# Seven block products for the up projection as well, and whole-block factors for the down projection

## The reference

```python
h = rms_norm(x, norm_ffn[l])                                  # 512 x 1024
x = x + jnp.square(jax.nn.relu(h @ w_up[l])) @ w_down[l]      # w_up 1024 x 4096, w_down 4096 x 1024
```

## Time and profile before

| | |
|---|---|
| median of three runs | 967.56 us |
| the profiled execution's own time | 967.63 us |
| its span, first to last instruction | 965.8 us |
| TensorE busy, matmuls | 954.9 us, 99% of the span, 4624 of them |
| VectorE busy | 599.3 us, 62% |
| ScalarE busy | 486.2 us, 50% |
| GpSimd busy | 168.6 us, 17% |
| moved by DMA | 116.18 MB, mean 120 GB/s |
| mean granted clock of TensorE | 0.999 |

### The profile page before, as it was taken

How to read it: one execution, slowest core, us unless ns; L and a number is a source line. 1 busy time by engine, 2 the same in 40 slices (tenths; PEclk the granted TensorE clock), 3 DMA queues, 4 the chain that set the end, 5 groups by cost and what they waited for, 6 DMA issues and landing times.

```text
span 965.8 us, 11653 instructions
## 1 busy us (share of the span) xinstructions
PE 954.9 (99%) x4624; PEld 789.6 (82%) x4624; DVE 599.3 (62%) x758; ACT 486.2 (50%) x735; POOL 168.6 (17%) x90
## 2 busy tenths in 40 slices
PE   9999999999999999999999999999999999999997
PEld 5888789888888888888888887898888888888885
DVE  5675523687468558657748752446855874685585
ACT  5566424653453454355455663356435534534543
POOL 2554215000010000000146434131000000100000
PEclk9999999999999999999999999999999999999999
DMA  9332114445534435544243311154454455345342
GB/s 297 136 110 88 55 55 139 122 110 160 167 80 117 175 87 129 194 113 89 88 137 131 110 67 66 44 175 90 129 207 98 88 164 163 80 117 175 87 88 88
DMA packets 33431, 116.18 MB, mean 120 GB/s; under 512 B 4832, under 2 KB 4960, under 8 KB 33376
## 3 DMA queue, kind: packets, MB, share of 16 engines
q1 hardware_dynamic: 28480, 98.06, 30.0%
q0 software_dynamic: 4608, 16.78, 10.6%
q10 hardware_dynamic: 288, 0.59, 0.2%
HBM read 113.32 MB, written 2.10 MB: 119 GB/s over the span
## 4 chain that ended last, share of the span: by engine, by line
PE 88%; DVE 7%; issue 3%; ACT 2%; POOL 0%; DVEq 0%; ACTq 0%
PE bank L489 16%; PE bank L491 16%; PE bank L490 16%; PE bank L486 12%; PE bank L488 11%; PE bank L487 11%; DVE rawx L1330 2%; DVE wlo L1077 1%; PE bank L511 1%; DVE rawx L1322 1%; DVE xt L1343 1%; PE bank L691 1%; PE bank L630 1%; PE bank L665 1%; PE bank L675 1%
## 5 line engine op out<-in xcount | busy, mean ns | idle before, releaser
L489 PE MATMUL bank<-xhi,wlo 128*128 128x512 f32 (+1 forms) x720 | 271.7, 377 | 0.0
L491 PE MATMUL bank<-xlo,whi 128*128 128x512 f32 (+1 forms) x720 | 270.1, 375 | 0.0
L490 PE MATMUL bank<-xhi,whi 128*128 128x512 f32 (+1 forms) x720 | 270.0, 375 | 0.0
L800 ACT ACTIVATE whi<-raw 128x1024 fp32r<-128x1024 f32 x172 | 181.1, 1055 | 131.5 <-PE bank L488 110.6
L455 POOL TENSOR_TENSOR wlo<-raw,whi 128x1024 fp32r<-128x1024 f32 x52 | 140.5, 2713 | 211.9 <-ACT whi L800 211.9
L486 PE MATMUL bank<-wlo,fhi 128*128 128x512 f32 x448 | 175.2, 391 | 2.2 <-DVE xt L1343 2.2
L1077 DVE TENSOR_TENSOR wlo<-raw,whi 128x1024 fp32r<-128x1024 f32 x120 | 145.9, 1221 | 50.6 <-ACT whi L800 50.6
L488 PE MATMUL bank<-whi,flo 128*128 128x512 f32 x448 | 174.4, 389 | 0.0
L487 PE MATMUL bank<-whi,fhi 128*128 128x512 f32 x448 | 174.3, 389 | 0.0
L489 PEld LDWEIGHTS bank<-xhi,wlo 128*128 128x128 f32 x720 | 135.6, 188 | 24.6 <-issue 0.3
L491 PEld LDWEIGHTS bank<-xlo,whi 128*128 128x128 f32 x720 | 135.5, 188 | 24.5
(11 more groups left out here) (109 smaller groups left out, 952.4 us busy)
## 6 DMA issues: line engine op xcount, KB each, us to landing
raw<-weights_in SPq DMA_DIRECT2D x156, 512.0 KB, 3.3
raw<-weights_in POOLq DMA_DIRECT2D x32, 512.0 KB, 5.9
rawx<-weights_in SPq DMA_DIRECT2D x16, 512.0 KB, 5.2
xt<-x_in SPq DMA_DIRECT2D x4, 512.0 KB, 8.1
gbc<-gains_in SPq DMA_DIRECT2D x4, 512.0 KB, 5.4
out_t<-xt SPq DMA_DIRECT2D x3, 512.0 KB, 2.6
gbc<-gains_in ACTq DMA_DIRECT2D x1, 512.0 KB, 5.5
wst<-ws_in SPq DMA_DIRECT2D x2, 256.0 KB, 6.7
```

The source lines that it names most:

```text
L489: pe.matmul(o, wlo[:, s, wc], hi[:, tokens], start=first, stop=False, skip_group_check=on_sum)
L490: pe.matmul(o, whi[:, s, wc], hi[:, tokens], start=False, stop=False, skip_group_check=on_sum)
L491: return pe.matmul(o, whi[:, s, wc], lo[:, tokens], start=False, stop=last, skip_group_check=on_sum)
L800: act.activation(whi[:, n % SLOTS, :], raw_at(slot), ACT.Copy).then_inc(whi_ready, 1)
```

## The change

The up projection is made by the same seven block products. The left operand is the weights (hidden features), the right one the tokens, so a product has 48 matmuls that stream 256 tokens each, and two pieces; a quarter has 336. Its factors of the tokens (A11, A12, A22 and the sums S2 to S5) are made once a layer, before the first quarter: ScalarE copies the turned tiles in full precision to `xf`, `xs_make` (VectorE) makes four sums of 128 x 1024, `xs_high` (ScalarE) and `xs_low` (VectorE) split them. The results of a quarter appear in three pairs of banks; ScalarE copies M1, M7 and M1+M6 out of the banks (`copy_sum`), VectorE adds them to later products (`up_sum`), and then come relu and square. The weight sums of the up phase are made as those of the down phase are: two more adding DMAs for M7 and two for M5, and VectorE's `sum_m6` and `sum_m4`.

For down the factors are made as whole blocks of 128 x 1024 (`make`, `factor_high`, `factor_low`). The order of products is M1, M7, M6, M4, M5, M2, M3 as before in the down phase, and M1, M2, M7, M6, M4, M5, M3 in the up phase. M4's weights in the down phase come from an adding DMA (B21) instead of VectorE. There are six landing slots instead of eight, and M3's right block lands where M2's was.

`gbc`, `bias`, `wst` and `bsb` move to memory that the MLP uses too, so `bias` is loaded and a part of `wst` cleared once a layer, and the gain of the next norm is loaded after the last up phase.

```diff
-PRODUCT_SLOT = (0, 2, 6, 6, 0, 4, 2)
+RAW_SLOTS = 6
+PRODUCT_SLOT = (0, 4, 4, 2, 0, 2, 2)      # M1..M7
+SEQUENCE = ((M1, M2, M7, M6, M4, M5, M3), (M1, M7, M6, M4, M5, M2, M3))
...
@@ sync: loads @@
+            def load_block(l, q, ph, r, g):
+                before = divmod(phase(l, q, ph) - 1 - l * 2 * QUARTERS, 2)
+                if r == M3:
+                    wait_low(sp, nth(l, group_pos(q, ph, M2, g)))
+                    if ph == UP:
+                        sp.wait_ge(weights_summed, summed_weights(l, q, UP, M4, g))
+                elif q or ph:
+                    wait_low(sp, nth(l, group_pos(*before, {M1: M5, M7: M4, M2: M3}[r], g)))
...
@@ gpsimd: adding DMAs @@
-                    for i in range(5 if q == 0 else 0):
-                        low(nth(l, up_pos(q, i)))
-                    for r in (M7, M5):
-                        for g in range(2):
-                            add_b12(l, q, r, g)
+                    add_blocks(l, q, UP, M7)
+                    if q == 0:
+                        for r in (M1, M2):
+                            for g in range(2):
+                                low(nth(l, group_pos(0, UP, r, g)))
+                    add_blocks(l, q, UP, M5)
+                    add_blocks(l, q, DOWN, M7)
+                    add_blocks(l, q, DOWN, M5)
+                    add_blocks(l, q, DOWN, M4)
...
@@ tensor @@
+            def up_banks(l, q, r, h):
+                if r in (M6, M4):
+                    pe.wait_ge(up_copied, copied(l, q, ADDS_TO[r], h))
+                elif r == M5:
+                    pe.wait_ge(up_copied, copied(l, q, M6, h))
+                elif r == M3:
+                    pe.wait_ge(up_summed, summed_up(l, q, M5, h))
...
+                for m in range(PAIRS):
+                    h, part = divmod(m, 2)
...
+                    for kc in range(PAIRS):
+                        mm = three(o, hi[:, kc, :], lo[:, kc, :], n, ..., slice(0, HALF), ...)
+                    if part:
+                        mm.then_inc(w_used, 1)
...
                 for q in range(QUARTERS):
-                    for i in range(3 if q == 0 else 0, KC):
-                        up(l, q, i).then_inc(w_used, 1)
-                    for r in (M1, M7, M6, M4, M5):
+                    for r in SEQUENCE[UP]:
+                        up_product(l, q, r)
+                        if q == 0 and r == M1:
+                            turn(2 * l + 1, NT - 1)
+                    for r in SEQUENCE[DOWN][:5]:
                         product(l, q, r)
...
@@ scalar, in the order of its queue @@
+                xs_high(0)
+                xs_high(1)
                 for q in range(QUARTERS):
+                    if q:
+                        hi_up(q, M7, 0)
+                    copy_sum(q, M1, 0)
+                    hi_up(q, M7, 1)
+                    copy_sum(q, M1, 1)
+                    if q == 0:
+                        xs_high(2)
+                        xs_high(3)
+                    hi_up(q, M6, 0)
+                    hi_up(q, M6, 1)
+                    hidden(q, M2, 0)
+                    hi_up(q, M4, 0)
+                    hidden(q, M2, 1)
+                    hi_up(q, M4, 1)
+                    copy_sum(q, M7, 0)
+                    copy_sum(q, M7, 1)
+                    factor_high(q, M1)
+                    hi_up(q, M5, 0)
+                    hi_up(q, M5, 1)
+                    copy_sum(q, M6, 0)
+                    copy_sum(q, M6, 1)
+                    hi_up(q, M3, 0)
+                    hi_up(q, M3, 1)
+                    hidden(q, M4, 0)
+                    hi_down(q, M1, 0)
...
@@ vector, in the order of its queue @@
+                xs_make(0)
+                xs_make(1)
+                xs_make(2)
+                xs_low(0)
+                xs_make(3)
+                xs_low(1)
                 for q in range(QUARTERS):
+                    low_up(q, M7, 0)
+                    if q:
+                        add_both(q - 1, M3)
+                    sum_m6(q, UP, 0)
+                    low_up(q, M7, 1)
+                    sum_m6(q, UP, 1)
+                    if q == 0:
+                        xs_low(2)
+                    low_up(q, M6, 0)
+                    sum_m4(q, 0)
+                    low_up(q, M6, 1)
+                    sum_m4(q, 1)
+                    up_sum(q, M2, 0)
+                    if q == 0:
+                        xs_low(3)
+                    up_sum(q, M2, 1)
+                    low_up(q, M4, 0), low_up(q, M4, 1), factor_low(q, M1), low_up(q, M5, 0), low_up(q, M5, 1)
+                    low_up(q, M3, 0), low_up(q, M3, 1), up_sum(q, M4, 0), up_sum(q, M4, 1)
+                    low_down(q, M1, 0), up_sum(q, M5, 0), low_down(q, M1, 1), up_sum(q, M5, 1), make(q, 0)
+                    low_down(q, M7, 0), sum_m6(q, DOWN, 0), factor_low(q, M7), low_down(q, M7, 1), sum_m6(q, DOWN, 1)
+                    low_down(q, M6, 0), make(q, 1), make(q, 2), low_down(q, M6, 1)
                     add_both(q, M1)
+                    factor_low(q, M6), factor_low(q, M4)
                     low_down(q, M4, 0)
+                    add_both(q, M7)
+                    factor_low(q, M5)
                     low_down(q, M4, 1)
-                    add_both(q, M7)
                     low_down(q, M5, 0)
+                    factor_low(q, M2)
                     low_down(q, M5, 1)
                     add_both(q, M6)
                     low_down(q, M2, 0)
+                    make(q, 3)
+                    factor_low(q, M3)
                     low_down(q, M2, 1)
                     add_both(q, M4)
                     low_down(q, M3, 0)
                     low_down(q, M3, 1)
```

More of the change, by code:

```diff
@@ L1009, in a11_high @@
[L1009 to L1027 removed]
+                close_mixer(2 * l + 1, nth(l, MLP_POS))
@@ new lines, in xs_high, with copy_sum @@
+                def xs_high(i):
+                    made, src = ((1, s3), (3, xf[:, 0, :, :]), (2, xf[:, 3, :, :]), (4, xf[:, 1, :, :]))[i]
+                    act.wait_ge(xs_made, l * 4 + made)
+                    act.copy(factor_x((S3, S2, S5, S4)[i])[0], src).then_inc(xs_hi, 1)
+                def copy_sum(q, r, h):
+                    act.wait_ge(w_used, nth(l, group_pos(q, UP, r, h)) + 1)
+                    if r == M6:
+                        act.wait_ge(up_summed, summed_up(l, q, M2, h))
+                    to = both(xf[:, 2, 2 * h:2 * h + 2, :]) if r == M7 else first_sum[:, h, :]
+                    act.copy(to, bank(l, sum_bank(UP, r, h))[:, :]).then_inc(up_copied, 1)
```

572 lines of the change are left out of this document (350 added, 222 removed).

## The result

The changed kernel takes 998.72 us (median of 4 runs, 992.74 to 1001.4) against 967.57 for the kernel before: a ratio of 1.0312 [1.0276, 1.0348]. It is slower, by 31 us, and outside the range that I gave (954 to 976). Its runs also spread over 0.9%, where those of the kernel before agree within 0.04%.

The account below looks back on a forecast made before the run. Bound by TensorE's matmul count: 31.2 us saved, about 27 returning as waits. Per layer +5.0 - 3.45 - 3.45 - 0.3 = -2.2, two layers -4.4 from 967.63, so 963.3 us; range of 8 in 10, 954 to 976.

Parts of the forecast that it names:

- The pitch of 0.120 us: Up phase: matmuls of 256 columns follow each other at 0.1199 us, as already seen in the first quarter.
- the up phase of 40.3: Each new up phase: 336 matmuls take 40.29 us, making a quarter 3.65 us shorter if nothing is late.
- The first quarter's walk: First quarter of a layer: following VectorE's and ScalarE's queues gave 9.4 us of waits, 88.8 us, taken as 5.0 more.
- The 3.5 us ahead of M4: First quarter's up phase: TensorE waits 3.5 us for ScalarE's copy of M7 out of its bank, done at 187.8.
- The adding DMAs' landing: Down phase: an adding DMA lands after 5.9 us, so M4's weights land at about 50.7 and 53.8.
- the down chain: Down phase: VectorE's operations from M4's adding DMAs through M2's second low part (67.0) to M3's load and M5's add (73.25).
- M3's load stands almost alone in time: End of down: argument against rival 1; M3's second tile lands 3.3 us after issue, bounds 3.1 to 5.2.
- rival 1: Longer chain at down's end makes the kernel slower; decides from 0.55 us more a quarter; 971 to 978.5 us; chance 0.28.
- the likeliest case: Whole kernel: the walk as made, 963.3 us, own range 955 to 968; chance 0.50.
- the queue as a fixed cost: Down phase: M5's add stands behind M3's low part in VectorE's queue, 0.2 us late in a steady quarter.
- the clock: Rival 3: clock falls in the 4.4 us gap ahead of first-quarter M7; up to 2.3 us a layer, 968; chance 0.13.
- Rival 2: Whole MLP: nothing is late, 936.4 us; with the first quarters late alone, 955; chance 0.09 with this half form.

Follow-up runs that it names:

- e2: Changed kernel, with the next quarter's two adding DMAs for M7 issued only when down's M3 has landed: 989.87 us.
- s2: Changed kernel with the 64 adding DMAs of M7 and M5 made plain copies, down's M4 left adding (sums left out): 973.15 us.
- p1: Changed kernel with every adding DMA made a plain copy of the same rows (sums of weights left out): 961.74 us.
- q1: e9 with only the second of the next quarter's two M7 adding DMAs waiting for down's first M3 tile: 962.2 us.
- e9: e1 with the whole first quarter of a layer in the order in which TensorE needs things, nothing held back: 970.66 us.
- e1: Changed kernel with M5's adds put ahead of M3's low parts in VectorE's queue: 977.58 us.
- e7: Changed kernel with matmuls of no use ahead of M7 and M4 of the first quarter and ahead of each down M3: 991.76 us.
- e3: Changed kernel with 36 matmuls of no use ahead of M7 of a layer's first quarter: 995.27 us.
- p2: e9 with every adding DMA made a plain copy (sums left out): 951.74 us.
- b0: The kernel before with its 32 adding DMAs made plain copies (sums left out): 967.44 us.
- e10: e1 with the low parts of down's M5 weights made by GpSimd instead of VectorE: 989.02 us.

## Why the prediction was wrong

**Right.** The pitch of 0.120 us and the up phase of 40.3. The first quarter's walk: I had M7's start at 172.7, M4's at 187.8 and M3's at 200.2; they are 172.75, 187.85 and 200.25. The 3.5 us ahead of M4 became 1.88, for M7 ran partly at the lower clock and M6 ended later; the start did not move. The adding DMAs' landing (5.9 taken, a median of 6.2 measured; M4's second landed 53.9 us after the start of the up phase for 53.8), and the order of the down chain up to the issue of M3's second load (67.3 us in for 67.0 in layer 0's q1).

**Wrong, the main step: "M3's load stands almost alone in time".** The term was 3.3 us, the median of all loads of the kernel before, with 3.1 to 5.2 as bounds, and it stood for M3's second tile. In six of the eight quarters that tile took 4.2 to 5.7 us. The first tile, which goes out 4.6 us sooner and which the walk therefore had off the chain, took 7.5 to 9.1, so that it landed hardly sooner than the second. The wait ahead of M3 became 1.5 to 2.9 us in the middle quarters for 0.2, and 2.3 and 3.1 in the first for 0.65. I had counted that a quarter's DMA time would double for the adding DMAs, and set it aside in one sentence, without listing what is issued around the load: the next quarter's M7 adding DMAs (305.22 and 309.15) and the loads for its M1. Where neither is there, in the last quarters, M3's loads took 3.4 to 3.6 us; with M1's loads but without the adding DMAs (e2) 4.2 to 4.6 and 3.3 to 3.4. So it is the adding DMAs above all. This is the mechanism of rival 1, with its point of decision (0.55 us a quarter), but priced at 5.2 us at most. Four experiments bear it out from different sides: e2 takes two DMAs away from the load's side (9 us less), s2 makes the 64 cheaper (26 less), p1 all (37 less), q1 moves one (8 less than e9).

In the last quarters the load was as forecast, and the waits of 4.4 and 3.6 us for 2.95 come from the links ahead of it: the second load went out 69.3 and 67.6 us in for 67.0, in layer 0 behind an adding DMA of M4 that landed after 8.6 us.

p1 brings that term near my value (4.6 and 3.5 us in layer 0's q1). It takes 961.7 us where I forecast 963.3, and its stretches are 89.0, 78.4, 78.4, 83.1 where I had 89.1, 78.7, 78.7, 84.5. That is so close in part by luck, for p1 isn't quite the prediction's case: M4's copies land sooner, so that the last quarters wait 1.6 us ahead of M3 for 2.95, and against that stand falls of the clock that the likeliest case did not have. The walk through the queues was sound, and the DMA term mis-sized.

**Wrong, the second step: the queue as a fixed cost.** The walk had M5's add behind M3's low part and took it as 0.2 us of lateness. With M3's tiles late it passes the lateness on to TensorE, 18.8 us in seven of the eight quarters; e1 removes 21 by two moved lines, the clock's falls behind those waits among them.

**Wrong, the third: the clock.** I gave its fall one place, ahead of M7, and 0 to 2.3 us a layer. In after it falls seven times ahead of the tail, also behind waits of 1.9 to 4.4 us elsewhere, four of them ahead of M3 of down. Waits of 1.88, 2.34 and 2.83 us in the same run had no fall behind them. Windows of after at the second layer's M3 of up, whose wait was 1.86:

```profile
684.00:686.00 2.00, 2.00 (x15) 2.00 (x16) 0.56 (x1) 1.63 (x3) 0.00 (x0) 0.78 0.72 295
686.00:688.00 2.00, 2.00 (x11) 2.00 (x11) 2.00 (x3) 2.00 (x3) 0.00 (x0) 0.50 0.01 4
688.00:690.00 2.00, 2.00 (x17) 2.00 (x17) 1.97 (x3) 1.97 (x4) 0.00 (x0) 0.87 0.00 0
```

(0.22 + 0.50 + 0.13) x 2 = 1.7 us of full-speed time. All seven took some 17 us of it in the profiled run (a mean granted clock of 0.982 over 990.8 us, less the tail). By e7 only about 7 us of the 31 hang on them: where the clock stays full, the next wait is longer, as ahead of M4 in e3. I had asked what the gap that I foresaw would do to the clock, not what the rivals' gaps would.

**The sum.** After stands 35.4 us over the forecast (998.7 - 963.3; the forecast's own terms give 963.2). Of the 29.4 us of the profiled run, 12.1 are waits (37.6 for the 25.5 of the walk) and some 17 the lower clock; the other 6 are the spread. p1 shows all of it to hang on the adding, part of the falls included: in p1 the clock still falls at M7 of each first quarter, and nowhere else ahead of the tail. Rival 2 was rightly low: even p2, with cheap DMAs and the orders by need, takes 951.7 and not 936.4, and over 10 us of the difference are waits of its two first quarters.

**Open.** Why the runs of after differ by 9 us among themselves: with plain copies the spread is 0.1% and with dummies in the gaps it stays, so it comes with the adding DMAs; what differs in them from run to run was not read. That the adding DMAs take more of the engines is measured, why they do is not.

## What to carry to other kernels

Before a transfer enters a sum with the median of its kind, list what else is issued from about 6 us ahead of it to its landing (5.4 here), and add up the engines' time of all of it. Where a step needs two transfers, do it for each: here the one that went out 4.6 us sooner landed only about 1 us ahead of the other. Where such a transfer feeds one link of an engine's in-order queue, put what TensorE needs and what does not depend on it ahead of it. And an adding DMA is no free sum: it costs twice the engines' time of a plain copy, which shows only in a control with the same bytes and no adding.

## What the runs showed of the hardware

- An adding DMA of 512 KB held the 16 engines for 3.0 us (23.9% of 990.8 for 80) and landed after a median of 6.2; a plain copy of the same bytes held them for 1.5 (12.8% of 959.5) and landed after 4.2. In the kernel before it is the same: 10.6% of 965.8 for 32, 3.2 each, and 4.9% of 965.6 in b0, 1.5 each.
- A 512 KB load landed after 3.4 us with nothing beside it (last quarters of after), 4.2 to 4.6 with two other loads issued 2.3 and 4.6 us ahead (e2), and 7.5 to 9.1 with two adding DMAs besides (after).
- A two-operand VectorE operation of 1.22 us took 2.2 to 3.4 beside a GpSimd operation of the same kind, and GpSimd's next DMA issues stand behind it (e10).
- The granted clock fell to 1.2 GHz behind seven of the waits of 1.86 to 4.44 us, each time for 1.7 or 3.4 us of full-speed time, but not behind three others of 1.88, 2.34 and 2.83. Matmuls put in a gap kept it full but moved the fall to the next gap (e3).
- Halving the columns of a matmul cost nothing beyond what the kernel before had shown: 0.120 against 0.227 us, now over whole phases of 336 matmuls.
